# Recurrence of the second block: three streams of tiles begun a third of a tile apart, with empty rounds before a late piece

## What is computed

```python
def rwkv7_mixer(p, shift_mu, w0, w2, a0, a2, g2, k_k, k_a, r_k, lnx_g, lnx_b):
    ...
    xs = (to_dirs(r, r), to_dirs(decay[:, :, 0], decay[:, :, 1]),
          to_dirs(k_dir[:, :, 0], k_dir[:, :, 1]), to_dirs(v, v), to_dirs(kk, kk),
          to_dirs(kka[:, :, 0], kka[:, :, 1]))
    S0 = jnp.zeros((N_DIR, B, RWKV_HEADS, HEAD_DIM, HEAD_DIM), jnp.float32)
    _, ys = lax.scan(rwkv7_step, S0, xs)
    ys = ys.transpose(1, 2, 0, 3, 4)
    y = ys[0] + jnp.flip(ys[1], axis=1)
```

## Time and profile before

| What | Value |
|---|---|
| Median of 3 runs | 3746.38 us (3745.59 to 3747.65) |
| The profiled execution | 3748.78 us |
| Its span | 3747.0 us |
| Granted TensorE clock, mean | 0.981 |
| PE busy, whole span | 3460.5 us (92%) |
| DVE busy | 1433.5 us (38%) |
| ACT busy | 673.4 us (18%) |
| POOL busy | 77.9 us (2%) |
| The recurrence's tiles | 1777 to 2063 us, 286 us of the span |

### The profile page before, as it was taken

One profiled execution on the slowest core, in us unless ns is written; L12 is line 12 of the kernel. 1 busy time (PEld: TensorE's weight loads), 2 busy tenths in 40 slices (PEclk: granted clock), 3 DMA queues, 4 the chain that ended last, 5 costly groups with the idle time before them and its releaser, 6 DMA issues. The chain is left out here.

```text
span 3747.0 us, 57543 instructions
## 1 busy us (share of the span) xinstructions
PE 3460.5 (92%) x25148; PEld 2400.0 (64%) x25148; DVE 1433.5 (38%) x3009; ACT 673.4 (18%) x1483; POOL 77.9 (2%) x128
## 2 busy tenths in 40 slices
PE   8999999798898988899888899999999999999997
PEld 5877888333332333257676777878887856887666
DVE  2465455211011110134676344345523623534344
ACT  2217311100000000012342125112100001101231
POOL 0000000000000000000222000000000000000000
PEclk9999999999999999999999899999999999999999
DMA  6430121999999999930000310222222111221110
GB/s 243 157 145 14 46 90 56 395 428 428 428 427 426 423 427 427 427 138 1 4 4 4 107 35 23 79 82 90 86 72 90 68 68 68 68 90 38 50 63 23
DMA packets 125849, 593.82 MB, mean 158 GB/s; under 512 B 7296, under 2 KB 37632, under 8 KB 99232
## 3 DMA queue, kind: packets, MB, share of 16 engines
q1 hardware_dynamic: 125600, 590.14, 39.5%
HBM read 588.02 MB, written 2.10 MB: 157 GB/s over the span
## 5 line engine op out<-in xcount | busy, mean ns | idle before, releaser
L2742 PE MATMUL banks<-slabs,ring 128*128 128x256 f32 (+1 forms) x3912 | 872.9, 382 | 0.2 <-DVE ring L2893 0.2
L2742 PEld LDWEIGHTS banks<-slabs,ring 128*128 128x128 f32 x3912 | 740.6, 190 | 117.3 <-issue 10.5
L2100 PE MATMUL banks<-ring,slabs 128*64 128x512 f32 x2304 | 516.7, 596 | 84.0 <-DMA ring<-in_w_exp 72.0
L2100 PEld LDWEIGHTS banks<-ring,slabs 128*64 128x64 f32 x2304 | 162.8, 137 | 413.6 <-issue 319.5
L393 PE MATMUL banks<-slabs,ring 128*128 128x264 f32 (+3 forms) x1224 | 344.9, 439 | 6.0 <-PEq L323 2.5
L393 PEld LDWEIGHTS banks<-slabs,ring 128*128 128x128 f32 (+1 forms) x1224 | 229.7, 191 | 104.2 <-issue 67.9
L2237 DVE TENSOR_TENSOR work<-work,banks 128x512 f32<-128x512 f32 x32 | 22.0, 688 | 488.8 <-PE banks L2100 488.8
L2742 PE MATMUL banks<-ring 128*128 128x256 f32 (+1 forms) x848 | 197.6, 381 | 0.9 <-PEq L323 0.7
L2100 PE MATMUL banks<-slabs 128*64 128x512 f32 x768 | 171.9, 596 | 21.3 <-DMA slabs<-in_w_exp 18.4
L2742 PEld LDWEIGHTS banks<-ring 128*128 128x128 f32 x848 | 160.1, 190 | 26.8 <-issue 4.5
L2987 PE MATMUL banks<-slabs,ring 128*128 128x264 f32 x768 | 172.4, 386 | 1.6 <-issue 1.6
(11 more groups left out here) (566 smaller groups left out, 4058.8 us busy)
## 6 DMA issues: line engine op xcount, KB each, us to landing
ring<-in_w_exp SPq DMA_DIRECT2D x144, 2048.0 KB, 15.8
slabs<-in_w_exp SPq DMA_DIRECT2D x48, 2048.0 KB, 32.1
ring<-in_w_in SPq DMA_DIRECT2D x19, 2048.0 KB, 11.8
ring<-in_w_ff SPq DMA_DIRECT2D x16, 2048.0 KB, 8.3
ring<-in_even_w_in SPq DMA_DIRECT2D x14, 2048.0 KB, 8.0
ring<-in_w_ada SPq DMA_DIRECT2D x12, 2048.0 KB, 10.7
ring<-in_w_out SPq DMA_DIRECT2D x4, 2048.0 KB, 8.0
ring<-in_even_w_out SPq DMA_DIRECT2D x4, 2048.0 KB, 8.0
```

Source lines behind the costliest of these rows:

```text
L2100: ins = mm(out[64 * c:64 * c + CAP, :], lhsT[:, k, :], w[:, at:at + 512], start=first and k == 0, stop=last and k == 3)
L2742: last = mm(bank, a[:, k, :], b[:, k, :], start=k == 0, stop=k == h - 1)
```

## The change

The streams start at rounds 0, 4 and 9 in place of 0, 1 and 2. The planner now works out the round in which each piece's factors begin while it hands out tiles, and a tile whose newest piece is 2 or 3 is moved back, if need be, to the twelfth round after that piece's factors began; the stream has empty rounds until then. All four engines' generators yield those empty rounds. No instruction is added, removed or resized; the order in which each engine's program goes through them changes.

```diff
-TILE_STEPS = 14
+TILE_STEPS, PRE_STEPS, READY_STEP = 14, 15, 12
...
     def __init__(self, pieces, streams):
-        free = list(range(streams))
+        free = [TILE_STEPS * i // streams for i in range(streams)]
         self.start, self.jobs, self.tiles = list(free), [[] for _ in free], []
+        self.factors_at = [None, 0]
...
         for parts in order:
-            i = free.index(min(free))
-            self.jobs[i].append(parts)
-            free[i] += TILE_STEPS
+            i, newest = free.index(min(free)), max(p for p, _, _, _ in parts)
+            while len(self.factors_at) <= newest:
+                n = len(self.factors_at)
+                self.factors_at.append(max(self.factors_at[-1] + PRE_STEPS if n >= 3 else 0, ends[n - 2] + 1))
+            empty = max(0, self.factors_at[newest] + READY_STEP - free[i]) if newest >= 2 else 0
+            self.jobs[i].append((parts, empty))
+            free[i] += TILE_STEPS + empty
             for p, _, _, _ in parts:
...
         if p:
-            pre_at.append(max(pre_at[-1] + PRE_STEPS if p >= 2 else 0, plan.done[p - 2] + 1 if p >= 2 else 0))
+            pre_at.append(plan.factors_at[p])
...
                 yield from idle_until(0, start)
-                for i, parts in enumerate(jobs):
+                for i, (parts, empty) in enumerate(jobs):
+                    yield from idle_until(0, empty)
```

More of the change, by code:

```diff
@@ L3195, in in_rounds @@
             yield
-PRE_STEPS = 15
 class Factors(Side):
```

## The result

The changed kernel takes 3769.8 us (four runs, 3765.8 to 3772.1) where the kernel before takes 3747.0: a ratio of 1.0058 with a 95% interval of 1.0046 to 1.0070. The profiled execution is 3765.8 us long, its span 3764.0, so it is the mildest of the four. I had forecast 3748 us and a range up to 3761.

A forecast was written before the change was run, and what follows sets the result against it. PE's own work was taken as the bound. Rows 1 to 3 -1.5, rows 4 to 6 -4, factors +2, start +3, end +2 made +1.5 us on the median 3746.4, about 3748; range 3736 to 3761 for 8 in 10.

The forecast's parts named there:

- the pile-up: Crowded rounds where three streams' dense steps meet cost 5.9 us a plain row; half returns in rows 1 to 3: -3.0 each.
- cover: PE work of the other streams during long waits after steps 0 and 13; spreading loses +2.5 to 3 us a row.
- Rows 4 to 6: Second half of the recurrence, two streams one round apart, third five away: +0.7 waits, -2.0 pile-up, -4 us for three rows.
- the end: Streams 1 and 2 finish in rounds 92 and 93 without stream 0: +2 us, bounds 0 and +3.
- Start: Stream 0 alone with the factors for four rounds: +3 us by round 9, bounds +1 and +6.
- Factors: Rounds ending at "ready", where factors have 12 rounds and tile steps beside them change: +2 us, between -3 and +6.
- rival D: Factors late again, so streams bunch at "ready" and rows 4 to 6 stay as before: +5.5, 3752 us; chance 0.10.
- The stage alone moved: No stage outside the recurrence was to move by more than 1 us.
- DVE's answer: After step 0's issue ends, DVE's answer was to let PE go on 2.75 us later, unchanged.
- The wait for L3698: PE's wait at L3506 for DVE after step 0, streams 1 and 2: from 6.0 us to over 12.
- The uncovered rest: Part of the answer to step 0 left uncovered by the other streams: 1.8 us, three times a row.
- Rival B: Steps 0 lose their cover, the pile-up's cost stays, nothing is given back: +16.6, 3763 us; chance 0.27.

The follow-up runs named there:

- starts 0, 1, 6: Changed kernel's planner with streams starting at rounds 0, 1 and 6: 3760.9 us, 1.0029 of the kernel before.
- 0, 2, 4: Changed kernel's planner with streams starting at rounds 0, 2 and 4: 3760.1 us, 1.0035 of the kernel before.
- the plan with a bunched start and the hole behind it: Changed kernel with starts 0, 1, 2, then 3 and 7 empty rounds on streams 1 and 2 before their second tiles: 3772.0 us, 1.0062 of the kernel before.
- The empty rounds alone: Kernel before, starts kept, with three empty rounds before stream 0's fourth tile and four before stream 2's fifth: 3754.9 us, ratio 1.0017.
- the earlier answer: DVE's identity addition moved behind its PSUM reads: on the kernel before 3741.8 us (0.9986), on the changed kernel 3756.7 us (1.0023 of the kernel before).

## Why the prediction failed

**The step that failed is the pile-up.** "I take half in rows 1 to 3, as both causes are weakened and neither is removed: -3.0 a row, with +2.5 for cover -0.5." In row 2 the waits other than mid-step stops went from 2.2 us to 5.7, so cover cost 3.5 and not 2.5. But the sign came from the other term, the 3.0 us to come back, and hardly anything came back. Of its two parts, mid-step stops in row 2 fell from 4.3 to 3.8 us (over the stage from 18.6 to 14.3), and the clock went the other way, in row 2 from 3.3 to 6.4 us at 1.2 GHz, over the stage from 34 to 61. PE's busy time in the row grew by 1.5. I had written in the same paragraph that "a lone wait of 1.8 us is as long as those ahead of a drop now", and then priced the clock as a gain.

That the pile-up was 5.9 us a row is right by luck. The stops and the clock's part of row 2, 4.3 and 1.7, make 6.0. But I had got there as 41.5 less 35.6, with 30.1 for the steps, for which PE was busy for 33.1 without the clock's part, and with over 5 for waits that were 2.2: two errors of 3 us that cancel. (Two slips beside it: 30.1 and 5.2 make 35.3, not 35.6, and by the earlier trace rows the drop came at 1838.0, not 1837.5.)

Why the same waits bring more low time when they are spread is not shown. I think that in the bunch long steps of the three streams fall together, so that waits are few and PE has a store of steps after each, and that spread out they come one by one into a PE with nothing stored. No run separates this from the plain fact that there are more waits for the answer, 14 where there were 8.

**Rows 4 to 6: -4 forecast.** By stream 0's marks they take 147.4 us where they took 142.4, so +5.0; with the same false credit. These rows hold the end too, for which +2 was forecast. Their spacing 1, 5, 8 is that of starts 0, 1, 6, a plan that proved no better than 0, 2, 4.

**Start, +3 (bounds +1 and +6).** 6.0 us at the 750th matmul, at the upper bound. PE runs at 1.2 GHz until 1793 where it came out of it at 1787. But the plan with a bunched start and the hole behind it was no faster.

**Factors, +2 (bounds -3 and +6), and rival D.** The empty rounds alone cost 1.0017, some 6 us, at the upper bound. The waits at "ready" shrank, from 3.9 and 2.9 to 2.5 and 2.5, so D is out.

**Steps that held.** The stage alone moved. DVE's answer takes 2.65 us from its first operation to PE's step (1837.58 to 1840.23), where it was 2.60 (1791.00 to 1793.60). From the end of step 0's issue it is 3.00 here and was 2.75, as DVE began 0.35 us behind that end. The wait for L3698 more than doubled. The uncovered rest was smaller than the 1.8 forecast: the 14 waits have a mean of 1.3 us, from 0.7 to 2.0, and at four of the 18 tiles the profile shows none.

**Rival B.** Its sum, +16.6 us with "lone waits bring the half clock all the same", lies nearest: 17.0 us by the profile, 22.8 by the medians. Its chance was 0.27, and the range ended at 3761, two microseconds short of its 3763 and nine short of the median measured. B had the sign and the cause of the sign, that little is given back. That its size fits is partly luck: its sum is made of waits and empty rounds only, while PE's idle time grew by 5.5 us and its busy time, with the same instructions, by 13.0. No rival priced the low clock as a loss. A part of B leant on a rule. The Trainium skill, page "Runtime: NRT & Kernel Launch", section "Instruction fetch mechanics", says that instruction fetch is hidden. This case's traces disagree for steps this dense: stops, most of them 128 matmuls or a multiple of it apart, remain in every one, 14 to 23 us of "issue" in the stage. B's own reading, that the order of the steps wins few of them back, came near, with 4.3 of 18.6 us gone.

**How the loss divides.** By the profile, 12 to 13 of the 17.8 us are busy time and the rest is idle time; twice the added busy time is about the added low time, 27 us. By experiment, one wide matmul in the wait makes the changed kernel 0.26% faster with a low time about that of the kernel before, so that at least that much, nearly half of the 0.58%, is the clock, if the filling helps by nothing else and as far as ratios of two batches can be compared. With the earlier answer it is 0.35% faster, which takes off waits and clock together. The two kernels with the earlier answer still lie 0.37% apart. That rest may be the waits that are left, step 13's chain and the empty rounds; I did not separate it, so the larger part of the loss is not divided by experiment.

## What to carry over

An offset between streams is worth what the other streams have to do in the longest wait, not how even the load gets. Counting cover step by step gave the difference in a plain row nearly (3.0 us against 3.5), but not its level, and it missed for starts 0, 1 and 6, so test such a plan before trusting it. A wait that nothing covers can cost twice in this kernel, by itself and by the lower clock behind it; so price the clock on the side of the loss. And hold a hand working against the busy and idle time of the row that it is for, each by itself: a right sum can be two errors. Before moving streams about, shorten the answer: one operation moved behind the last PSUM read gave 0.15% with no change of plan.

## What was not expected

Less time at 1.2 GHz did not always bring time. In the changed kernel halving it (61 to 30 us) went with 10 us less; in the kernel before, 20 us less of it went with no gain (1.0006). The filling was hidden in the one and mostly not in the other, so that this does not show that a stretch at 1.2 GHz can be free.

The time that four small matmuls and one wide one take on PE is about the same, and they gave 0.05% and 0.26% (1.0053 and 1.0032, with intervals that overlap). Their low times differ as well, so that the cause is open.
